# Row norms split between ScalarE and VectorE, roots on VectorE, and the last norm made tile by tile inside the last projection

## The reference, cut to what matters

```python
def rms_norm(x, g):
    xf = x.astype(F32)
    y = xf * lax.rsqrt(jnp.mean(xf * xf, axis=-1, keepdims=True) + EPS)
    return (y * g.astype(F32)).astype(x.dtype)
...
hn = rms_norm(h, norm_mix[i])
h = h + forgetting_attention(hn, ...)      # i == 0
h = h + retention(hn, ...)                 # i == 1
```

## Time and profile before

| what | us |
|---|---|
| median of 3 runs | 3350.32 |
| lowest and highest | 3346.73, 3352.61 |
| the profiled execution | 3346.29 |
| its span, first to last instruction or transfer | 3344.5 |

### The profile page before, as it was taken

How to read it: one execution, slowest core, us unless ns; L and a number is a source line. 1 busy time by engine, 2 the same in 40 slices (tenths; PEclk the granted TensorE clock), 3 DMA queues, 4 the chain that set the end, 5 groups by cost and what they waited for, 6 DMA issues and landing times. The chain is left out here.

```text
span 3344.5 us, 30732 instructions
## 1 busy us (share of the span) xinstructions
PE 2847.3 (85%) x12394; PEld 1426.5 (43%) x12394; DVE 839.7 (25%) x2159; ACT 643.0 (19%) x1388; POOL 192.8 (6%) x144
## 2 busy tenths in 40 slices
PE   7999949778867999998588777489999997999997
PEld 3454533222223444444332222146655564555554
DVE  1130421101102202112211110323714443054044
ACT  2220410000001000001000000213503342142143
POOL 1000010000000000000100000110010102012001
PEclk9999959999998999998699999799999998999999
DMA  5502059999984333224699999701001011121100
GB/s 186 232 26 76 26 216 380 427 427 427 428 335 170 125 115 112 101 75 176 244 428 427 427 427 428 277 25 34 1 27 39 13 51 48 51 73 48 51 23 32
DMA packets 117647, 604.84 MB, mean 181 GB/s; under 512 B 9701, under 2 KB 23978, under 8 KB 92794
## 3 DMA queue, kind: packets, MB, share of 16 engines
q1 hardware_dynamic: 91632, 537.15, 39.8%
q10 hardware_dynamic: 20618, 46.89, 4.0%
q0 software_dynamic: 5248, 18.75, 1.5%
HBM read 559.17 MB, written 43.52 MB: 180 GB/s over the span
## 5 line engine op out<-in xcount | busy, mean ns | idle before, releaser
L479 PE MATMUL psum<-ring,XT 128*128 128x512 f32 (+3 forms) x1216 | 480.2, 555 | 14.7 <-ACT arena L1705 6.6
L469 PE MATMUL psum<-XT,ring 128*128 128x512 f32 (+1 forms) x1152 | 444.2, 547 | 2.8 <-DVEq L2078 2.8
L1061 PE MATMUL psum<-arena 128*64 128x512 f32 x1280 | 306.1, 624 | 114.0 <-DMA arena<-in_expert_w_gu 113.8
L479 PEld LDWEIGHTS psum<-ring,XT 128*128 128x128 f32 x1216 | 230.2, 190 | 256.4 <-issue 222.4
L469 PEld LDWEIGHTS psum<-XT,ring 128*128 128x128 f32 x1152 | 219.3, 191 | 226.8 <-issue 215.6
L561 PE MATMUL psum<-ring,arena 128*128 128x512 f32 x704 | 306.1, 593 | 8.5 <-DVEq L2078 4.2
L1061 PE MATMUL psum<-ring,arena 128*64 128x512 f32 x768 | 191.5, 646 | 70.0 <-DMA ring<-in_expert_w_gu 67.2
L686 PE MATMUL psum<-arena 64*128 64x384 f32 (+8 forms) x704 | 221.1, 500 | 27.1 <-ACT arena L740 22.1
L1061 PEld LDWEIGHTS psum<-arena 128*64 128x64 f32 x1280 | 91.5, 142 | 300.2 <-issue 172.9
L1131 DVE TENSOR_TENSOR arena<-arena,psum 64x512 f32<-64x512 f32 x64 | 44.1, 689 | 692.4 <-ACT arena L1134 692.4
L561 PEld LDWEIGHTS psum<-ring,arena 128*128 128x128 f32 x704 | 132.2, 190 | 171.9 <-issue 159.3
(11 more groups left out here) (246 smaller groups left out, 2323.5 us busy)
## 6 DMA issues: line engine op xcount, KB each, us to landing
arena<-in_expert_w_gu SPq DMA_DIRECT2D x80, 2048.0 KB, 24.7
ring<-in_expert_w_gu SPq DMA_DIRECT2D x48, 2048.0 KB, 24.6
arena<-in_expert_w_down SPq DMA_DIRECT2D x40, 2048.0 KB, 28.1
ring<-in_expert_w_down SPq DMA_DIRECT2D x24, 2048.0 KB, 28.1
ring<-in_ada_w SPq DMA_DIRECT2D x12, 2048.0 KB, 9.3
ring<-in_fox_w_in SPq DMA_DIRECT2D x8, 2048.0 KB, 8.4
arena<-xg_dram ACTq DMA_DIRECT2D x32, 512.0 KB, 10.3
y_dram<-arena ACTq DMA_DIRECT2D x128, 128.0 KB, 8.6
```

The source lines that it names most:

```text
L469: i = pe.matmul(ps[0][0:cols_[1] - cols_[0], 0:ntok], w[:, c, cols_[0]:cols_[1]], x[:, c, tok:tok + ntok], start=(c == 0), stop=(c == k - 1))
L479: i = pe.matmul(ps[0][:, 0:width], x[:, c, t * P:(t + 1) * P], w[:, c, c0:c0 + width], start=(c == 0), stop=(c == k - 1))
L1061: i = pe.matmul(psum[side * BR:(side + 1) * BR, 0:FF], x[:, 4 * part + c, :], w[:, c, side * FF:(side + 1) * FF], start=(part == 0 and c = ...
```

## The change: what it does

`SplitNorm` replaces `Norm` in `n0`, `n1`, `m10` and `m11`: ScalarE squares the even tiles, VectorE the odd ones (tensor_tensor_reduce with a summed output); the root is made by VectorE alone with `root_of`; and TensorE begins when the first two tiles are scaled: it transposes tiles 0 and 1 of all 8 chunks, then tiles 2 and 3 of all 8 chunks, and signals `turned` only in the second round. `LastProj` replaces `OutProj` in `oc1`, and the stage `last` goes: ScalarE loads the gain at the head of the stage and squares each tile as soon as both its halves are summed, VectorE makes the root and the scaled tile (`made`) for tile 0 ahead of job 4, for tile 1 ahead of job 6, and for tiles 2 and 3 behind job 7, and SP issues the stores.

```diff
--- before.py
+++ after.py
                     i.then_inc(self.s("turned"), 1)
 
+        class SplitNorm(Norm):
+
+            def totals(self):
+                v = self.tiles // 2
+                return dict(squares=1, rstd=1, rows_a=self.tiles - v, rows_v=v, turned=self.chunks, out_a=self.chunks // 2)
+
+            def act(self, act):
+                even = range(0, self.tiles, 2)
+                for t in even:
+                    i = act.activation(self.junk, self.rows[:, t, :], ACT.Square, accum_out=st[:, 0, t:t + 1])
+                    if t < even[-1]:
+                        act_step.then(act, i)
+                i.then_inc(self.s("squares"), 1)
+                act.wait_ge(self.s("rstd"), self.at("rstd") + 1)
+                for t in even:
+                    act.activation(self.scaled[:, t, :], self.rows[:, t, :], ACT.Copy, scale=st[:, 3, t:t + 1])\
+                        .then_inc(self.s("rows_a"), 1)
+                for c in range(0, self.chunks, 2):
+                    act.wait_ge(self.s("turned"), self.at("turned") + c + 1)
+                    act.activation(self.out(c), bank(c, self.tiles * P), ACT.Identity,
+                                   scale=self.gain(c), bias=self.shift(c) if self.shift else 0.0).then_inc(self.s("out_a"), 1)
+
+            def dve(self, dve):
+                n = self.tiles
+                junk = region(5120, D)
+                for t in range(1, n, 2):
+                    dve_step.then(dve, dve.tensor_tensor_reduce(junk, self.rows[:, t, :], self.rows[:, t, :], 1.0, 0.0,
+                                                                ALU.mult, ALU.add, st[:, 0, t:t + 1]))
+                ms, t_, y, r = (st[:, j, 0:n] for j in range(4))
+                dve.wait_ge(self.s("squares"), self.at("squares") + 1)
+                dve_step.then(dve, dve.tensor_scalar(ms, ms, 1.0 / self.width, EPS, ALU.mult, ALU.add))
+                root_of(dve, ms, y, t_, r)
+                dve.nop().then_inc(self.s("rstd"), 1)
+                for t in range(1, n, 2):
+                    dve.tensor_scalar(self.scaled[:, t, :], self.rows[:, t, :], st[:, 3, t:t + 1], None, ALU.mult)\
+                        .then_inc(self.s("rows_v"), 1)
+                for c in range(1, self.chunks, 2):
+                    dve.wait_ge(self.s("turned"), self.at("turned") + c + 1)
+                    if self.shift:
+                        dve.tensor_scalar(self.out(c), bank(c, n * P), self.gain(c), self.shift(c), ALU.mult, ALU.add)
+                    else:
+                        dve.tensor_scalar(self.out(c), bank(c, n * P), self.gain(c), None, ALU.mult)
+
+            def pe(self, pe):
+                for t0 in range(0, self.tiles, 2):
+                    pe.wait_ge(self.s("rows_a"), self.at("rows_a") + t0 // 2 + 1)
+                    pe.wait_ge(self.s("rows_v"), self.at("rows_v") + t0 // 2 + 1)
+                    for c in range(self.chunks):
+                        for t in range(t0, t0 + 2):
+                            i = pe.transpose(bank(c)[:, t * P:(t + 1) * P], self.scaled[:, t, c * P:(c + 1) * P], ident)
+                        if t0 + 2 == self.tiles:
+                            i.then_inc(self.s("turned"), 1)
...
+            def between(self, dve, n):
+                pass
...
                 for n, (t, half) in enumerate(self.jobs()):
+                    self.between(dve, n)
                     dve.wait_ge(self.s("filled"), self.at("filled") + n + 1)
...
-        class RowNorm(Stage):
-
-            kind = "rownorm"
-
...
+        class LastProj(OutProj):
+
+            Y, G, JUNK = region(4096, NT, D), region(8192, D), region(9216, D)
 
             def act(self, act):
-                act.dma_start(self.g, self.gain.partition_broadcast(P)).then_inc(self.s("gain"), 16)
-                squares(self, act, [H[:, t, :] for t in range(NT)], region(8192, D))
-                if self.out_ is not None:
-                    for t in range(NT):
-                        act.wait_ge(self.s("made"), self.at("made") + t + 1)
-                        act.dma_start(self.out_[0, t * P:(t + 1) * P, :], self.y[:, t, :]).then_inc(self.s("stored"), 16)
-                    act.wait_ge(self.s("stored"), self.at("stored") + 16 * NT)
+                act.dma_start(self.G, io["final_g_2"].partition_broadcast(P)).then_inc(sem("last_gain"), 16)
+                super().act(act)
+                for t in range(NT):
+                    act.wait_ge(self.s("summed"), self.at("summed") + 2 * t + 2)
+                    if t:
+                        act.wait_ge(sem("last_squared"), t)
+                    act.activation(self.JUNK, H[:, t, :], ACT.Square, accum_out=st[:, 0, t:t + 1]).then_inc(sem("last_squared"), 1)
+
+            def sp(self, sp):
+                Weights.load(sp, self.unit)
+                for t in range(NT):
+                    sp.wait_ge(sem("last_made"), t + 1)
+                    sp.dma_start(io["out"][0, t * P:(t + 1) * P, :], self.Y[:, t, :]).then_inc(sem("last_stored"), 16)
+                sp.wait_ge(sem("last_stored"), 16 * NT)
+
+            def made(self, dve, t):
+                ms, tmp, y, r = (st[:, j, t:t + 1] for j in range(4))
+                dve.wait_ge(sem("last_squared"), t + 1)
+                dve_step.then(dve, dve.tensor_scalar(ms, ms, 1.0 / D, EPS, ALU.mult, ALU.add))
+                root_of(dve, ms, y, tmp, r)
+                dve.scalar_tensor_tensor(self.Y[:, t, :], H[:, t, :], r, self.G, ALU.mult, ALU.mult).then_inc(sem("last_made"), 1)
+
+            def between(self, dve, n):
+                if n == 0:
+                    dve.wait_ge(sem("last_gain"), 16)
+                if n % 2 == 0 and n >= 4:
+                    self.made(dve, n // 2 - 2)
 
             def dve(self, dve):
-                inverse_roots(self, dve, NT, D)
-                dve.wait_ge(self.s("gain"), self.at("gain") + 16)
-                for t in range(NT):
-                    dst = H[:, t, :] if self.out_ is None else self.y[:, t, :]
-                    dve.scalar_tensor_tensor(dst, H[:, t, :], st[:, 3, t:t + 1], self.g, ALU.mult, ALU.mult)\
-                        .then_inc(self.s("made"), 1)
+                super().dve(dve)
+                for t in range(NT - 2, NT):
+                    self.made(dve, t)
 
...
-            norm = Norm("n0", H, D, NT, gain_cols(V_MIX), None, XT, 0, region(0, NT, D))
+            norm = SplitNorm("n0", H, D, NT, gain_cols(V_MIX), None, XT, 0, region(0, NT, D))
...
-            Norm("n1", H, D, NT, gain_cols(V_MIX + KC), None, XT, 0, region(0, NT, D))
+            SplitNorm("n1", H, D, NT, gain_cols(V_MIX + KC), None, XT, 0, region(0, NT, D))
...
             for g, (rows, tiles, tok0) in enumerate(((H, NT, 0), (HC, NCT, SEQ))):
-                Norm(f"m{layer}{g}", rows, D, tiles, lambda c, g=g: amod[:, layer, c, g:g + 1],
+                SplitNorm(f"m{layer}{g}", rows, D, tiles, lambda c, g=g: amod[:, layer, c, g:g + 1],
                      lambda c, g=g: modc[:, layer, c, g:g + 1], XT, tok0, region(0, NT, D))
 
...
-                use_units(OutProj(f"oc{g}", u, 4, ZT, NT, 1), u)
+                if g:
+                    LastProj(f"oc{g}", u, 4, ZT, NT, 1).unit = u
+                else:
+                    use_units(OutProj(f"oc{g}", u, 4, ZT, NT, 1), u)
 
         parts = [lambda: Start("start"), fox, lambda: moe(0, free_in_fox), retention, lambda: moe(1, free_in_retention),
                  lambda: TwoNorms("nfin"), mixer_a, mixer_b,
-                 lambda: mod_norms(1), mixer_c, lambda: RowNorm("last", io["final_g_2"], io["out"])]
+                 lambda: mod_norms(1), mixer_c]
```

7 lines of the change are left out of this document (removed).

## The result

| | kernel before | changed kernel |
|---|---|---|
| median (us), lowest to highest, runs | 3350.17, 3342.69 to 3352.61, 5 | 3325.96, 3321.54 to 3328.28, 5 |
| ratio, with 95% interval | | 0.9932 (0.9919 to 0.9944) |
| the profiled execution, its span | 3346.29, 3344.5 | 3321.54, 3319.8 |
| mean granted clock of the span | 0.949 | 0.952 |

The account below looks back on a forecast made before the run. TensorE, busy 85% of the span, bounds the kernel; norms pay only where it idles. 5.5 + 0.4 + 6.8 = 12.7 us off 3346.29 or 3350.3 gives 3333.6 or 3337.6, forecast 3336, range 3332 to 3340, with two rivals 3330 to 3343.

Parts of the forecast that it names:

- The squares: Four-tile norms: two squares on VectorE beside two on ScalarE, 2.53 us instead of 4.83, saving 2.30 three times.
- The root: Norms: 11 small VectorE instructions plus a signalling nop, 2.22 us against 2.21 with ScalarE's square root, a draw.
- The rule weighed against it: Each ScalarE table switch costs about 2.66 us, 1.38 a drain; 1.4 us more saved per norm, 4 in all; not adopted.
- The start of the transposes: Four-tile norms: first transpose 6.14 us after the first square, where it was 9.48.
- The end: After the last gated product: last tile scaled at 3334.15 instead of 3341.0, saving 6.8 us.
- rival (c): Last projection: VectorE's SBUF work stretches GpSimd's adds to 5.9 us or more, 3357 and more; chance 0.03.
- Rival (b): Norms: VectorE's squares don't run beside ScalarE's, so norms gain nothing and lose 0.5 us each in drains; 3344, chance 0.09.
- Drains: Four-tile norms, first transpose to last drain: 7.3 us if clock rises early, 7.95 if late, 5.80 before in `n1`.
- The early start buys nothing: Four-tile norms: starting transposes earlier wins 1.05 us, but about 1.5 is lost by the last drain.
- Rival (a): Behind the norms: TensorE's longer pause lowers the clock, costing 3 to 4.4 us in all; 3340 to 3341, chance 0.22.
- Rival (d): `m11` and the stage behind it: half clock ends earlier relative to work, 2 to 4 us more, 3333; chance 0.06.
- the sum: Whole kernel: 5.5 us in `n0`, `n1`, `m10`, 0.4 in `m11`, 6.8 at the end, 12.7 us saved.

Follow-up runs that it names:

- e8_root_by_scalar: Changed kernel with the root made by ScalarE's square root again in the four split norms; 3325.03 us (4 runs).
- e3_one_round: Changed kernel, but TensorE waits for all scaled tiles and transposes chunk by chunk in one round, as before the change; 3325.19 us.
- e6_two_more_norms: Changed kernel with the two norms ahead of the experts (`nf0`, `nf1`) split as well; 3326.69 us.
- e10_before_warm: Kernel before, with unread TensorE matmuls (11, or 7 in `m11`) during squares and root in `n0`, `n1`, `m10`, `m11`; 3341.47 us, ratio 0.9989.
- e1_end_only: Kernel before with only `LastProj` (last norm per tile in the last projection), all other norms as before; mean 3339.0 us, ratio 0.9985.
- e2_norms_only: Kernel before with only the four split norms, the last norm still a stage of its own; mean 3333.8 us, ratio 0.9964.
- e11_last_mixer_norms: Kernel before with only `m10` and `m11` split, `n0`, `n1` and the end as before; 3340.57 us (11 runs).
- e7_warm: Changed kernel with 7 unread TensorE matmuls at the head of each of the four split norms; 3323.36 us.
- e4_late_by_one: Changed kernel with one more, unread square of a tile on ScalarE in `n0`; 3327.68 us.

## Why the prediction was wrong, step by step

**The steps that held.** The squares: first small instruction 2.47 us behind the first square in `n0`, 2.66 in `n1`, 2.59 in `m10`; forecast 2.53. The root: a draw forecast (2.22 against 2.21), 2.23 to 2.24 measured. The rule weighed against it, of the Trainium skill ("ScalarE: Activation LUTs", What ACT_TABLE_LOAD costs), would have given 4 us more by the prediction's estimate; `e8_root_by_scalar` contradicts it here, since with the table load back in, the stages get no longer. There the load took 1.28 us and ScalarE's next instruction started 0.01 us behind it (1007.51 + 1.28, then 1008.80), so the drain of that rule doesn't show. The start of the transposes: 6.10, 6.30 and 6.22 us, forecast 6.14. The end: 6.7 saved, 6.8 forecast. Its details differ a little: tiles 2 and 3 took 7.54 us, not 6.95, since one small instruction of tile 2 (L350) took 1.07 us instead of 0.16, until GpSimd's add had ended; the store gave 0.4 back (3.1 us from the last scaling to the span's end, 3.5 before). Ahead of it the tiles made between the products cost nothing: TensorE's last 56 matmuls took 24.20 us, in the trace of before as in this. Of rival (c) a trace exists in that one instruction, on VectorE's side; GpSimd's add stayed at 1.26 us. Rival (b) is out: VectorE's first square starts 0.13 us behind ScalarE's.

**Drains.** First transpose to last drain was forecast at 7.3 (early rise) and 7.95 (late). `n1` took 7.25, `m10` 7.77, `n0` 6.91. In `n0` and `n1` the four odd drains took 2.73 and 2.72 us and not 3.37: three drains that each wait for a chunk had taken 2.50, and I scaled that row up to four, but drains that find all their chunks ready go at 0.66 us apiece. `e3_one_round` shows the two paces side by side. "The early start buys nothing" was wrong by 0.7 to 1.4 us in `n0` and `n1`. This term is about 1 us of the 10. That `n1` came out at its 7.3 is luck, two errors that cancel: the clock rose about 4.2 us into its transposes and not 3, so the first odd drain began 4.53 us behind the first transpose instead of 3.92.

```profile
1017.00:1018.00 1.00, 1.00 (x8) 1.00 (x7) 0.22 (x1) 0.64 (x1) 0.00 (x0) 0.68 1.06 389
```

**Rival (a)** did not happen. TensorE's pause ahead of the next stage grew from 1.02 to 1.68 us in `n1` and to 1.74 in `n0`, not to 2.5, since the transposes themselves lasted longer (5.82 and 5.46 us instead of 5.0). The windows behind the two pauses:

```profile
27.90:30.00 2.10, 2.09 (x5) 0.48 (x6) 0.00 (x0) 0.00 (x0) 2.10 (x1) 1.00 1.05 386
1020.70:1023.00 2.30, 2.25 (x6) 1.09 (x7) 0.00 (x0) 0.00 (x0) 1.16 (x2) 1.00 1.00 311
```

The clock is at its full level in both, as forecast.

**Rival (d)** happened. The projection behind `m11` starts at full clock; the windows of before, then of after:

```profile
2816.00:2818.00 2.00, 2.00 (x3) 0.91 (x4) 0.00 (x0) 0.00 (x0) 0.00 (x0) 0.50 0.45 108
```

```profile
2801.00:2803.00 2.00, 2.00 (x6) 0.89 (x5) 0.00 (x0) 0.00 (x0) 0.00 (x0) 1.00 0.62 161
```

Six matmuls instead of three pass in 2 us. It is about 2 us, in seven of the eight traces of the changed kernel and its variants with all split norms and the new end (not in `e6_two_more_norms`), but not with the norms alone (1.9 still lost) nor with the last mixer's alone (1.9); so it isn't a property of the split, and what decides it in the changed kernel stays open. `e10_before_warm` has it without the split, by TensorE's unread work. Read from that first matmul to the program's last, the stretch took 510.7 and 510.2 us before, 510.3 with the end alone (`e1_end_only`), and 508.0 and 507.9 in the changed kernel. That is 2.5 us, 2.3 of them in its first 146 us, which rival (d) had priced at 2 to 4 and given a chance of 0.06.

**The step that failed is the sum.** It took 12.7 us off a base that was too high and put everything outside the four places at nothing, the stage behind `m11` too. Of the 10 us between 3336 and 3326:

- 3.2 are the base. I took off 12.7 from 3348.7, between the profiled execution (3346.3) and the median of three (3350.3). 56 runs have a mean of 3345.5. A median of three of a kernel that scatters by 3.5 us was no reason to go up.
- 1.3 are the stages: 14.0 seen in the mean of both pairs, 12.7 summed.
- 5.5 (19.5 - 14.0), give or take 2, lie outside the four stages. `e1_end_only` excludes the end (6.5 measured, 6.7 in its stage). `e2_norms_only` (11.7 against 7.4) and `e11_last_mixer_norms` (4.5 against 2.7) point to the norms, though `e2_norms_only` only just and `e11_last_mixer_norms` within its error.

Of the 5.5 us, 2.5 are rival (d), the stage behind `m11`. The other 3 stay open. A guess is that half clock falls less in the mixers a and b, but no single place shows it. Here are the same 8 matmuls behind the same pause, in the first trace of before, the second one, and the changed kernel:

```profile
2567.71 5.43 PE L686 MATMUL psum<-arena 96*128 96x512 f32 x8 [2.24 <-ACT arena L740]
```

```profile
2563.90 4.32 PE L686 MATMUL psum<-arena 96*128 96x512 f32 x8 [2.24 <-ACT arena L740]
```

```profile
2556.38 4.54 PE L745 MATMUL psum<-arena 96*128 96x512 f32 x8 [2.24 <-ACT arena L799]
```

The second trace of before has the short time as well, and `e2_norms_only` and `e7_warm`, with split norms, have 5.49: it is a draw. Over the mixers a and b the five traces with the old `n0` and `n1` lost 10.2 to 15.9 us (mean 13.8), the nine with split ones 8.0 to 11.8 (mean 10.5): 3.3 us less. Most of that comes from the 257 us between the pause of the earlier trace rows and the matmuls just shown: this stretch is 256.7 and 256.9 us long in the two traces of before, 260.0 to 260.1 in the other three of the five, and 256.6 to 258.5 in the nine. The forgetting attention goes the other way (mean loss 0.6 with the old norms, 2.6 with the new). All told the loss outside the experts and outside `m10` and `m11` is 43.6 in the mean of the five and 40.5 in that of the nine, 3.1 us less, with traces of equal code 5 to 8 us apart: not shown. A part may also be the stages themselves: over all traces that have a stage in either form the four save 14.9 us and not 14.0. Why the half clock comes at the same places of the code and lasts 1.5 us in one execution and 3 in another, or is absent, stays open. Unread matmuls moved it where they stood and right behind (`e7_warm`, `e10_before_warm`); nothing here moved it at will elsewhere, and `e4_late_by_one`, which shifts everything by 1.4 us, leaves the mixers' loss at 10.2.

## What to carry to other kernels

Sum a change by the stage's own time and check it against that stage in the trace: here four sums of a few microseconds each came out within 1.4 us, while one pair of spans was off by 11. Price also the stage behind each that you change: putting it at nothing missed 2.5 us here. Before a difference of spans is explained, take a second trace of the same code and the time that each lost to the half clock; two executions of one kernel differed by 6 us in span and 8 in that loss, as much as a whole part of this change. When work is reordered so that several drains are ready at once, time them as a queue of ready ones, not by rows in which each waited for its producer.
